# Experts: gathering the token rows in rounded float32, as a rounded part and a rest

## The reference, cut to what matters

```python
logits = (xt @ router_w + router_b).astype(jnp.float32)   # xt: 256 tokens x 1024
top_v, top_e = lax.top_k(logits, TOP_K)                    # 4 of 32 experts for each token
gates = jax.nn.softmax(top_v, axis=-1)
...
def expert_block(args):
    xblk, e = args                                         # the tokens that chose expert e
    act = clamped_swiglu(xblk @ w1[e] + b1[e])             # 1024 -> 2 x 1024 -> 1024
    return act @ w2[e] + b2[e]                             # 1024 -> 1024
```

## Time and profile before

| | |
|---|---|
| median of 3 runs | 2445.81 us (2444.83 to 2446.50) |
| profiled execution | 2451.43 us |
| its span, from the first to the last instruction | 2449.6 us |
| granted TensorE clock, mean | 0.992 |
| PE busy | 2345.6 us (96%) |
| DVE busy | 1348.8 us (55%) |
| ScalarE (ACT) busy | 983.8 us (40%) |
| moved by DMA | 673.90 MB, mean 275 GB/s |

### The profile page before, as it was taken

One profiled execution on the slowest core, in us unless ns is written; L12 is line 12 of the kernel. 1 busy time (PEld: TensorE's weight loads), 2 busy tenths in 40 slices (PEclk: granted clock), 3 DMA queues, 4 the chain that ended last, 5 costly groups with the idle time before them and its releaser, 6 DMA issues.

```text
span 2449.6 us, 36827 instructions
## 1 busy us (share of the span) xinstructions
PE 2345.6 (96%) x13938; PEld 1643.0 (67%) x13939; DVE 1348.8 (55%) x2652; ACT 983.8 (40%) x1789; POOL 95.7 (4%) x150
## 2 busy tenths in 40 slices
PE   6999999999999999999999999999999999999999
PEld 3777854444444444444448888888888888987888
DVE  5688752222223222222347868877677666665785
ACT  3645541111111111111136545655555566566653
POOL 1000000000000000000000000100000201011000
PEclk8999999999999999999999999999999999999999
DMA  8764679999999999999975555555555655553553
GB/s 320 252 217 145 237 289 426 427 428 428 428 428 428 428 428 428 428 427 428 428 303 175 182 193 173 184 184 175 185 190 173 195 163 160 155 163 114 192 180 119
DMA packets 270842, 673.90 MB, mean 275 GB/s; under 512 B 8885, under 2 KB 236608, under 8 KB 246017
## 3 DMA queue, kind: packets, MB, share of 16 engines
q1 hardware_dynamic: 266464, 663.60, 71.4%
q0 software_dynamic: 4256, 8.65, 1.6%
HBM read 670.45 MB, written 1.25 MB: 274 GB/s over the span
## 4 chain that ended last, share of the span: by engine, by line
PE 85%; DVE 7%; ACT 4%; issue 3%; DMA 1%; DVEq 0%; ACTq 0%; SPq 0%
PE PS L380 26%; PE PS L1499 18%; PE PS L381 13%; PE PS L1520 9%; PE PS L1482 5%; PE PS L1469 3%; PE PS L387 2%; PE PS L388 2%; PE PS L389 2%; DVE WS L328 2%; ACT WS L324 1%; DVE XG L1615 1%; PE PS L800 1%; DMA RAW<-in_w_ada 1%; PE PS L2169 1%
## 5 line engine op out<-in xcount | busy, mean ns | idle before, releaser
L380 PE MATMUL PS<-HN,WS 128*128 128x512 f32 x1952 | 702.9, 403 | 15.0 <-DVE WS L328 8.3
L328 DVE TENSOR_TENSOR WS<-RAW,WS 128x1024 fp32r<-128x1024 f32 (+1 forms) x452 | 542.2, 1205 | 166.9 <-ACT WS L324 162.4
L381 PE MATMUL PS<-HN,WS 128*128 128x256 f32 x1952 | 549.5, 282 | 0.0
L324 ACT ACTIVATE WS<-RAW 128x1024 fp32r<-128x1024 f32 (+1 forms) x452 | 465.4, 1035 | 101.1 <-PE PS L381 69.1
L1499 PE MATMUL PS<-RING,XG 128*64 128x512 f32 x2048 | 446.5, 594 | 10.9 <-DVE XG L1615 10.9
L380 PEld LDWEIGHTS PS<-HN,WS 128*128 128x128 f32 x1952 | 370.0, 190 | 109.3 <-DVE WS L328 10.2
L381 PEld LDWEIGHTS PS<-HN,WS 128*128 128x128 f32 x1952 | 372.2, 191 | 0.3
L1499 PEld LDWEIGHTS PS<-RING,XG 128*64 128x64 f32 x2048 | 149.2, 137 | 293.9 <-issue 293.9
L1621 DVE TENSOR_SCALAR GLU<-PS 128x256 f32<-128x256 f32 x64 | 27.2, 425 | 413.3 <-PE PS L1499 413.3
L380 PE MATMUL PS<-MI,WS 128*128 128x512 f32 x704 | 248.5, 398 | 0.0
L1520 PE MATMUL PS<-RING,AT 128*64 128x512 f32 x1024 | 226.8, 594 | 14.8 <-ACT AT L1391 14.8
(11 more groups left out here) (363 smaller groups left out, 2676.0 us busy)
## 6 DMA issues: line engine op xcount, KB each, us to landing
RING<-in_moe_w SPq DMA_DIRECT2D x192, 2048.0 KB, 21.4
RAW<-in_ffn_w_in SPq DMA_DIRECT2D x88, 1024.0 KB, 5.2
RAW<-in_attn_w_qkv SPq DMA_DIRECT2D x36, 1024.0 KB, 5.2
RAW<-in_ffn_w_out SPq DMA_DIRECT2D x32, 1024.0 KB, 5.0
RAW<-in_w_ada SPq DMA_DIRECT2D x24, 1024.0 KB, 8.1
RAW<-in_w_in SPq DMA_DIRECT2D x22, 1024.0 KB, 5.3
RAW<-in_ffn_w_out SPq DMA_DIRECT2D x16, 768.0 KB, 4.3
RAW<-in_conv_w_in SPq DMA_DIRECT2D x12, 1024.0 KB, 5.1
```

Of the source, the lines that this page charges most:

```text
L324: act_f(split_tile(0, n), raw_tile(n), ACT.Copy).then_inc(hi_done, 1)
L328: vec.tensor_tensor(split_tile(1, n), raw_tile(n), split_tile(0, n).bitcast(f32), ALU.subtract).then_inc(lo_done, 1)
L380: nc.tensor.matmul(both, hi[:, k, :], x2[:, :, kx, :], start=start, stop=False)
L381: ins = nc.tensor.matmul(half, lo[:, k, :], x2[:, 0, kx, :], start=False, stop=stop)
```

## The change

H2K and PSEL get the rounded type. ScalarE's copy to H2K thereby rounds. DVE computes the rest of each piece (the PSUM value times the token's root, less the rounded value) into a new tile H2L, also rounded: lower_rows, two operations a piece. The first piece's call stands after L1569, the other three after L1588, before the loop. The gather multiplies both H2K and H2L with PSEL, into the same sum. PE waits for h_low (the four calls) instead of h_ready. H2L lies where SQR was, which is read early in the routing.

```diff
-    H2K = rw("H2K", [TT, D])
+    H2K = rw("H2K", [TT, D], f32r)
...
-    PSEL = rw("PSEL", [TT, SLOTS])
+    PSEL = rw("PSEL", [TT, SLOTS], f32r)
...
+    H2L = Region(ub0)("H2L", [TT, D], f32r)
...
-            pe.wait_ge(sem("h_ready"), 4)
+            pe.wait_ge(sem("h_low"), 4)
...
                     for k in range(DC):
                         for tt in range(TT):
-                            last = nc.tensor.matmul(bank[4][:, k * SLOTS:(k + 1) * SLOTS], H2K[:, tt, k * P:(k + 1) * P],
-                                                    PSEL[:, tt, :], start=tt == 0, stop=tt == TT - 1)
+                            for rows in (H2K, H2L):
+                                last = nc.tensor.matmul(bank[4][:, k * SLOTS:(k + 1) * SLOTS], rows[:, tt, k * P:(k + 1) * P],
+                                                        PSEL[:, tt, :], start=tt == 0 and rows is H2K,
+                                                        stop=tt == TT - 1 and rows is H2L)
...
+            def lower_rows(i):
+
+                m = H_TURNED[i]
+                dve.wait_ge(sem("h_ready"), i + 1)
+                for q in range(2):
+                    o2 = 512 * (m % 2) + 256 * q
+                    hi, lo = (t[:, m // 2, o2:o2 + 256].rearrange("p (k x) -> p x k", k=2) for t in (H2K, H2L))
+                    last = STT(lo, bank[m][:, 256 * q:256 * (q + 1)].rearrange("p (x k) -> p x k", k=2), RSC[:, 1, m // 2:m // 2 + 1],
+                               hi.bitcast(f32), ALU.mult, ALU.subtract)
+                last.then_inc(sem("h_low"), 1)
...
             o.mark(TS(ONEH[:, :, :], MSK[:, :, :], 4096.0, -4096.0, ALU.mult, ALU.add))
+            lower_rows(0)
             dve.wait_ge(sem("top_exp"), TT)
...
             vec.memset(STAT[:, 6, :], 0.0).then_inc(sem("gat_ready"), 1)
+            for i in range(1, 4):
+                lower_rows(i)
             dve.wait_ge(sem("blocks_ready"), 1)
```

## The result

The change made the kernel slower: 2494.8 us median of 4 runs (2493.3 to 2500.1) against 2446.2 us, a ratio of 1.0189, 95% interval 1.0165 to 1.0213 (the two medians alone give 1.0199). The forecast was 2492.6 us.

The account below looks back on a forecast made before the run. TensorE was taken to set the expert stage's pace, weight transfers close behind. Late start 2.5 us plus clock falls 44.3 us made 46.8 us, added to 2445.8 us: 2492.6 us, range 2446 to 2501 us.

Parts of the forecast that it names:

- main term: TensorE in the expert blocks: clock falls to 1.2 GHz after 27 of 32 gathers, 1.64 us each, 44 us; chance 0.55.
- the rival case of a steady clock: TensorE's clock holds through the blocks, leaving only the 2.5 us late start: 2448.3 us; chance 0.26.
- The gather's loads: Gather on TensorE: still 32 weight loads a block at 0.112 us each, 3.6 us, so no time saved.
- that rival: Gather's rounded weights load quicker, saving TensorE 85 us, but transfers become the bound: 2446.0 us; chance 0.06.
- DVE's work: Before the first block: two lower_rows operations hidden, six at 0.46 us, so the first gather starts 2.5 us later, once.
- The reason given for the falls: Each gather: array without columns 2.7 of 3.6 us, then 0.34 us waiting for XG, more empty time than before either earlier fall.
- The transfers: Weight transfers in the expert stage: held back by TensorE's releases, close behind it; landing times stay near those before.
- The bound of 2.3 us: End of the expert stage: the transfers' lead left, the most the kernel can keep of TensorE's savings over 32 blocks.

Follow-up runs that it names:

- e1_wide: Changed kernel with each gather matmul except the last chunk's streaming PSEL's 64 columns twice; 2455.7 us, ratio 1.0032 to the kernel before.
- e3_narrow: Kernel before, plain float32, with the gather's products for the second half of the tokens taking 8 columns instead of 64; 2486.4 us, ratio 1.0148.
- e4_half: Changed kernel with only the rounded part H2K in the gather, 16 matmuls a block instead of 32; ratio 0.9999 to the kernel before.
- e7_part: Changed kernel without lower_rows, gathering only rounded H2K, 16 matmuls a block, PE waiting for h_ready; 2443.2 us, ratio 0.9970 to the kernel before.

## Why the prediction was right

Its main term, falls of the clock after the gathers, came as it said: 25 of them for 27, where the gathers end. Its range, 2446 to 2501 us, held the rival case of a steady clock too, so the time alone tells little; the falls in the trace do.

**The gather's loads** were as it said: 32 at 0.112 us, before and after, and with twice the columns. The Trainium skill (TensorE: Matmul & The Clock Gate, "Weight-path perf modes — Fast Weight Load (FWL) and DoubleRow") speeds up loads of 128 columns whose type isn't FP32; the rounded loads, at the same 0.112 us as the plain ones, show nothing of it, so that rival fell. That columns don't set the 0.112 is shown (64 and 128 take the same); that it is the load, and not something else that each instruction costs, is argued from the rows of PEld.

**DVE's work** was in the main as it said: the first two operations hidden in the idle time, and 2.5 us of delay. Its six operations took 3.01 us from 340.73 to 343.74, 0.50 each and not 0.46, so the copies came 2.67 us later after ONEH (6.80 instead of 4.13). The start moved by 9.34 - 6.83 = 2.51 us, since 0.16 us was made up between the copies and the gather: the 2.5 came out so exactly by luck.

**The falls** were forecast as 27 of 1.64 us, 44.3 us. There were 25 short ones in the blocks, and they cost (41.4 - 2.8) / 25 = 1.54 us each, 38.6 us. The ones that begin 4.6 us or more after the gather's start cost 1.7 us, as in a dense layer; those at 3.7 to 3.9 us cost 1.2 to 1.3. The early ones reach over the wait for XG, which, it seems, a slow clock doesn't lengthen.

**The reason given for the falls** was right in what it named, too few columns in the gather, and wrong in how it measured that. The prediction added the gather's time without columns to the wait for XG, found more than the 1.94 and 1.76 us of the two falls, and so expected falls. The kernel before has 1.9 + 0.34 = 2.2 us by the same sum, more than both too, and its clock held through all 32 gathers. The sum doesn't tell the two kernels apart; e1_wide and e3_narrow do.

**One term was left out.** The prediction made TensorE wait 2.5 us longer before the first block and priced that as delay alone, although its own rows had falls after waits of 1.94 and 1.76 us. That wait had its own low stretch, which cost 2.8 us. With it the three terms are 2.5 + 2.8 + 38.6 = 43.9 us. The forecast 46.8 was nearer to the measured 48.6 than this by luck: the other 4.7 us of the profiled run lie before and after, where the change has no part. The run e3_narrow, which has nothing of the change ahead of the gather, had its ONEH 2.5 us later than the kernel before, too.

**The transfers** behaved as drawn: slowed by TensorE they keep their lead, a piece landing 10.6 us after its issue from 1150 to 1210 us. Against a faster TensorE they close the lead and take over (e4_half, e7_part).

```profile
RING<-in_moe_w SPq DMA_DIRECT2D x12, 2048.0 KB, 10.6
```

The bound of 2.3 us on what could be kept was too low: the stage kept 3.3 to 3.5. The prediction left out that a shorter gather also lets the first pieces of the ring come free earlier, by 1.8 us at most; that this makes the difference is likely, but wasn't tried apart.

What stays open is why few columns bring the fall. The runs show that gathers with few columns are followed by it and gathers with many are not, at the same number and pace of instructions; but with the columns the array's multiplications and its writes to PSUM change too, and no run parts these.

## What to carry to other kernels

Before halving the work of a product, look at what sets its pace: here the load of the weights, so half the streaming time bought nothing. Then look at what the clock makes of it: here a stretch of small matmuls that the profile shows as fully busy was followed by a fall of the clock, and the bill came in the large products behind it. Wider matmuls, writing columns that nobody reads, cost nothing under these loads (3.48 us for the gather either way) and took the falls away; they win back what the change lost, and no more. And before saving TensorE's time in a stage that streams weights, work out the transfers' lead at its end: here 57 us saved on TensorE left 3.5.

## What was not expected

A wait of 2.8 us in front of a gather was enough for 6.8 us at half clock, in the changed kernel and with the plain gather alike (with half the gather, in e4_half, for 3.4), and this cost more than the wait had been lengthened by (2.8 against 2.5 us). The falls in the blocks came in a steady pattern, four blocks with and one without from the fifth block on; why every fifth block or so is spared wasn't tried. In the profile's slices of 62 us nothing of this is to be seen.
